# Long convolution by matrix DFT: transforms folded mod 4, its products shared between two engines, filter taps on row halves of the array

## What is computed

```python
def two_sided_fftconv(u, h_fwd, h_bwd):
    L = u.shape[1]
    filt = jnp.concatenate([h_fwd, jnp.zeros((1, h_fwd.shape[1]), F32), h_bwd[1:][::-1]], axis=0)
    filt_f = jnp.fft.rfft(filt, n=2 * L, axis=0)
    u_f = jnp.fft.rfft(u.astype(F32), n=2 * L, axis=1)
    y = jnp.fft.irfft(u_f * filt_f[None], n=2 * L, axis=1)[:, :L]
    return y.astype(u.dtype)

def hyena_mixer(u, w_in, b_in, conv_w, conv_b, f_w1, f_b1, f_freq1, f_w2, f_b2, f_freq2, f_w3, decay, d_bias, w_out, b_out):
    L = u.shape[1]
    z = dwconv3(u @ w_in + b_in, conv_w, conv_b)
    x1, x2, v = jnp.split(z, 3, axis=-1)
    h_fwd, h_bwd = hyena_filters(L, f_w1, f_b1, f_freq1, f_w2, f_b2, f_freq2, f_w3, decay)
    v = v * x2
    y = (two_sided_fftconv(v, h_fwd, h_bwd) + v * d_bias) * x1
    return y @ w_out + b_out
```

## Time and profile before

| | |
|---|---|
| median of three runs | 1707.78 us (1706.72 to 1708.12) |
| the profiled execution, its own time | 1708.62 us |
| its span | 1706.8 us |
| PE busy | 1686.2 us, 99% |
| DVE busy | 1038.0 us, 61% |
| POOL busy | 1019.2 us, 60% |
| ACT busy | 560.6 us, 33% |
| PE's granted clock, mean | 0.996 |

### The profile page before, as it was taken

One profiled execution on the slowest core, in us unless ns is written; L12 is line 12 of the kernel. 1 busy time (PEld: TensorE's weight loads), 2 busy tenths in 40 slices (PEclk: granted clock), 3 DMA queues, 4 the chain that ended last, 5 costly groups with the idle time before them and its releaser, 6 DMA issues.

```text
span 1706.8 us, 24447 instructions
## 1 busy us (share of the span) xinstructions
PE 1686.2 (99%) x9142; PEld 1402.0 (82%) x9142; DVE 1038.0 (61%) x1514; ACT 560.6 (33%) x1019; POOL 1019.2 (60%) x675
## 2 busy tenths in 40 slices
PE   9999999999999999999999999999999999999998
PEld 7778888788888887789888888888888898887887
DVE  3457767677777863445477637756548548846173
ACT  3557777624233232203223125232222221113111
POOL 3437676565666764555666175666667645557663
PEclk8999999999999999999999999999999999999999
DMA  9213233132259862343432133334443344222332
GB/s 357 78 56 108 100 105 103 35 111 76 94 201 314 289 224 92 125 147 120 165 99 87 37 100 100 118 122 153 143 134 121 126 161 150 86 74 93 99 99 87
DMA packets 56760, 217.20 MB, mean 127 GB/s; under 512 B 6305, under 2 KB 8609, under 8 KB 53346
## 3 DMA queue, kind: packets, MB, share of 16 engines
q1 hardware_dynamic: 51634, 201.80, 35.0%
q10 hardware_dynamic: 5040, 14.22, 2.2%
HBM read 201.84 MB, written 14.16 MB: 127 GB/s over the span
## 4 chain that ended last, share of the span: by engine, by line
PE 92%; DVE 4%; ACT 1%; POOL 1%; DMA 1%; issue 0%; SPq 0%; DVEq 0%; POOLq 0%; ACTq 0%
PE PS L2036 27%; PE PS L2037 26%; PE PS L2038 26%; PE PS L2367 2%; PE PS L2383 2%; PE PS L786 2%; PE PS L573 1%; PE PS L2190 1%; PE PS L1434 1%; DMA X<-in_x 0%; DVE WA L1634 0%; PE PS L1440 0%; POOL WL L1954 0%; POOL PR L1979 0%; PE PS L2105 0%
## 5 line engine op out<-in xcount | busy, mean ns | idle before, releaser
L1954 POOL TENSOR_TENSOR WL<-RAW,WH 128x1024 fp32r<-128x1024 f32 (+3 forms) x233 | 601.1, 2580 | 19.5
L2036 PE MATMUL PS<-HH,WH 128*128 128x512 f32 (+1 forms) x1400 | 529.5, 378 | 2.8 <-POOL WL L1954 1.1
L2038 PE MATMUL PS<-HH,WL 128*128 128x512 f32 (+1 forms) x1400 | 524.7, 375 | 0.0
L2037 PE MATMUL PS<-HL,WH 128*128 128x512 f32 (+1 forms) x1400 | 524.5, 375 | 0.0
L1951 POOL TENSOR_SCALAR WH<-RAW 128x1024 fp32r<-128x1024 f32 (+3 forms) x233 | 258.1, 1108 | 295.6 <-PE PS L2038 280.4
L2036 PEld LDWEIGHTS PS<-HH,WH 128*128 128x128 f32 x1400 | 263.6, 188 | 57.5 <-issue 10.1
L2038 PEld LDWEIGHTS PS<-HH,WL 128*128 128x128 f32 x1400 | 263.5, 188 | 47.7
L2037 PEld LDWEIGHTS PS<-HL,WH 128*128 128x128 f32 x1400 | 263.6, 188 | 45.8
L1950 POOL TENSOR_TENSOR SC<-ONES 1x1 f32<-1x1 f32 x134 | 32.1, 239 | 281.8 <-PE PS L2038 281.8
L1979 POOL TENSOR_SCALAR PR<-PR,SC 128x768 f32<-128x768 f32 x47 | 109.5, 2337 | 69.8 <-DVE SC L3080 69.8
L2036 PE MATMUL PS<-HIDH,WH 128*128 128x512 f32 (+1 forms) x396 | 148.4, 375 | 0.0
(11 more groups left out here) (435 smaller groups left out, 2778.8 us busy)
## 6 DMA issues: line engine op xcount, KB each, us to landing
RAW<-in_wup SPq DMA_DIRECT2D x88, 512.0 KB, 3.5
MRF<-in_modw SPq DMA_DIRECT2D x52, 512.0 KB, 4.6
RAW<-in_wdn SPq DMA_DIRECT2D x32, 704.0 KB, 4.1
MR<-in_modw SPq DMA_DIRECT2D x28, 512.0 KB, 3.5
RAW<-in_whin SPq DMA_DIRECT2D x28, 512.0 KB, 3.5
MK<-in_modk SPq DMA_DIRECT2D x8, 1024.0 KB, 9.9
RAW<-in_whead SPq DMA_DIRECT2D x8, 640.0 KB, 4.9
RAW<-in_wo SPq DMA_DIRECT2D x8, 512.0 KB, 3.5
```

The costliest lines, as they stand in the source:

```text
L1954: pool.tensor_tensor(WL[s][:, 0:n], raw[:, 0:n], WH[s][:, 0:n].bitcast(F32), ALU.subtract).then_inc(tile_split, 1)
L2036: pe.matmul(out, wh, xh, start=first, stop=False)
L2037: pe.matmul(out, wh, xl, start=False, stop=False)
L2038: return pe.matmul(out, wl, xh, start=False, stop=last)
```

## The change

The signal is folded mod 4. The four residues of the times 0, 2, 1, 3 mod 4 (RESIDUE) are transformed separately for 128 frequencies (`transform(c, odd)`: 4 x 1 x 3 matmuls), with one tile of cosines and sines (`vdft`) that is loaded once into DFT_RAW, split by POOL and kept in place 3. Sums and differences of these give the spectrum at all 512 frequencies (`even_sums`, `odd_sums`, `first_sums`). The multiplications by HS are shared: DVE has the second class (`second_class`), POOL the first (`first_class`), but for the last two sums of class 1; `joined` adds them. `mixed` gives eight sums per chunk that undo the folding, done by POOL for the first chunk and by DVE for the second. The inverse (`back(c, k)`) has the table G as stationary operand: 2 matmuls of 512 columns for each residue, with times on partitions; ACT copies the result to YT, and `turn_back` transposes it, 4 transposes for each of eight channel tiles. The output projection's first two tiles are interleaved with them, and the split of y for the first four channel tiles goes to UTH and UTL. From input tile 11 on ACT writes WH (`rounded`) and POOL only WL (`rest`). The four spectrum tiles are no longer in the ring of weights. For the filters, the two matmuls of a tap use 64 rows each: forward in bank 6, backward in bank 7; DVE windows both (the backward one to BACK in SBUF) and forms difference and sum. FW3N and the two ACT instructions that made it go. In the filter tiles the second half of the frequencies is in falling order.

```diff
 def input_at(n):
 
-    return FIRST_TILE["hyin"] + n + sum(n > m for m in SPECTRUM_AFTER)
+    return FIRST_TILE["hyin"] + n
...
+            sp.dma_start(DFT_RAW[:, :], a["vdft"]).then_inc(S["tab_in"], 16)
             for c in range(4):
                 ring("hyin", a["whin"], 4 + c)
                 sp.dma_start(HS[:, c, :, :].rearrange("p s n -> p (s n)"), d_hs[:, c, :]).then_inc(S["g_in"], 16)
-            for c in range(2):
-                ring("hyin", a["whin"], 8 + c)
-                sp.dma_start(G[:, 2 * c:2 * c + 2, :], a["idft"][:, 2 * c:2 * c + 2, :]).then_inc(S["g_in"], 16)
...
+            def rest(n):
+
+                t = input_at(n)
+                pool.wait_ge(tile_hi, t + 1)
+                pool.tensor_tensor(WL[place_of(t)][:, 0:D], RAW[t % 2][:, 0:D], WH[place_of(t)][:, 0:D].bitcast(F32),
+                                   ALU.subtract).then_inc(tile_split, 1)
+
+            def first_class(i, part):
+
+                hr1, hi1, x, y = HS[:, i, 0, :], HS[:, i, 1, :], SUM[i % 2][0][:, :], SUM[i % 2][1][:, :]
+                p, q = PROD[0][:, :], PROD[1][:, :]
+                if part == 0:
+                    pool.wait_ge(S["zd"], 5 * (i // 2) + 2 + i % 2)
...
+                    pool.tensor_tensor(p, x, hr1, ALU.mult).then_inc(S["cls"], 1)
+                    pool.tensor_tensor(q, y, hi1, ALU.mult).then_inc(S["cls"], 1)
+                if part == 1:
+                    pool.wait_ge(S["cls"], (CLASS_DONE[i - 1] if i else 0) + 2)
+                    pool.tensor_tensor(x, x, hi1, ALU.mult).then_inc(S["cls"], 1)
+                    pool.tensor_tensor(y, y, hr1, ALU.mult).then_inc(S["cls"], 1)
+                if part == 2:
+                    pool.wait_ge(S["cls"], CLASS_DONE[i] - 2)
+                    pool.tensor_tensor(hr1, p, q, ALU.subtract).then_inc(S["cls"], 1)
+                    pool.tensor_tensor(hi1, y, x, ALU.add).then_inc(S["cls"], 1)
...
+            rest(22)
+            first_class(2, 1)
+            rest(23)
+            first_class(2, 2)
+            for part in range(3):
+                first_class(3, part)
...
-                for half, w in enumerate((FW3, FW3N)):
-                    m = pe.matmul(bank(6 + half), H2T[:, times(k)], w[:, 512 * c:512 * c + 512], start=True, stop=True)
+                for half in range(2):
+                    r = slice(HID_F * half, HID_F * half + HID_F)
+                    m = pe.matmul(bank(6 + half), H2T[r, times(k)], FW3[r, 512 * c:512 * c + 512], start=True, stop=True)
...
-                ins = dve.tensor_tensor(bank(6), bank(6), WN[n % 2][:, :], ALU.mult)
+                dve.tensor_tensor(BACK[:, :], bank(7), WN[n % 2][:, :], ALU.mult)
+                link(dve.tensor_tensor(bank(6), bank(6), WN[n % 2][:, :], ALU.mult))
+                dve.tensor_tensor(bank(7), bank(6), BACK[:, :], ALU.subtract).then_inc(S["pq"], 1)
+                ins = dve.tensor_tensor(bank(6), bank(6), BACK[:, :], ALU.add)
...
-                dve.tensor_tensor(bank(7), bank(7), WN[n % 2][:, :], ALU.mult).then_inc(S["pq"], 1)
...
+                for b in (0, 2, 1, 3):
+                    k = 2 * odd + b % 2
+                    if c and not odd and b == 1:
+                        pe.wait_ge(S["zd"], 5)
+                    m = mm3(bank(2 + b), *chunk(DFT_PLACE, 4 * odd + b), UTH[:, k, :], UTL[:, k, :], True, True)
+                m.then_inc(S["dft"], 1)
+
+            def back(c, k):
+
+                pe.wait_ge(S["mix"], 8 * c + 4 * (k // 2) + 4)
...
+                for wave, x in enumerate(back_terms(c, k)):
+                    m = pe.matmul(bank(back_bank(c, k)), G[:, 2 * k + wave, :], x, start=wave == 0, stop=wave == 1)
+                m.then_inc(S["dft"], 1)
+
+            def turn_back(n):
...
+                pe.wait_ge(S["hcopy"], 8 + 4 * c + 4)
+                if n >= 2:
+                    pe.wait_ge(S["iev"], n - 1)
+                for k, r in enumerate(RESIDUE):
+                    m = pe.transpose(PS[:, 6 + n % 2, r * P:r * P + P], YT[c][:, k, ct * P:ct * P + P], IDENT[:, :])
+                m.then_inc(S["tv"], 1)
...
+            for k in range(4):
+                back(0, k)
+            back(1, 0)
+            back(1, 1)
+            turn_back(0)
+            turn_back(1)
+            back(1, 2)
+            back(1, 3)
+            turn_back(2)
+            turn_back(3)
+            for k in range(3):
+                out_step(0, k)
+            turn_back(4)
+            turn_back(5)
...
+            def rounded(n):
...
+                act.copy(WH[place_of(t)][:, 0:D], RAW[t % 2][:, 0:D]).then_inc(tile_hi, 1)
...
+            def mix():
+                dve.wait_ge(S["zd"], 10)
+                for n in range(8):
+                    out, x, y, op = mixed(1, n)
+                    dve.tensor_tensor(out, x, y, op).then_inc(S["mix"], 1)
+                    dve.wait_ge(S["mix"], 8 + n + 1)
...
             short_conv(22)
-            product(3, 0)
+            joined(2)
             short_conv(23)
-            product(3, 1)
-            product(3, 2)
+            joined(3)
+            mix()
             gated(0)
```

More of the change, by code:

```diff
@@ L553, in pool_hyena, with mix @@
+            def mix(n0, n1):
+                if n0 == 0:
+                    pool.wait_ge(S["zd"], 5)
+                for n in range(n0, n1):
+                    out, x, y, op = mixed(0, n)
+                    pool.tensor_tensor(out, x, y, op).then_inc(S["mix"], 1)
+                    pool.wait_ge(S["mix"], n + 1)
             for j in range(4):
                 split("hyin", j)
-            with pool.Fori(0, 12) as i:
-                for j in range(2):
-                    split("hyin", 4 + j, i, 2)
+            split("hyin", 4)
@@ new lines, in pool_hyena @@
+            dft_hi()
+            split("hyin", 5)
+            dft_lo()
+            with pool.Fori(0, 2) as i:
+                for j in range(2):
+                    split("hyin", 6 + j, i, 2)
+            split("hyin", 10)
+            for n in range(ROUNDED_BY_ACT, 14):
+                rest(n)
+            first_class(0, 0)
+            rest(14)
+            first_class(0, 1)
+            rest(15)
+            first_class(0, 2)
+            rest(16)
+            first_class(1, 0)
+            rest(17)
@@ L798, in pe_hyena @@
             turn_values(3)
+            transform(0, 0)
             into(10)
-            spectra(0)
-            for n in range(11, 15):
+            transform(0, 1)
+            for n in range(11, 17):
                 into(n)
-            spectra(1)
-            into(15)
-            into(16)
             turn_values(4)
@@ new lines, in odd_sums, with odd_banks, first_sums @@
+            def odd_sums(c):
+                dve.wait_ge(S["dft"], 2 * c + 2)
+                dve.wait_ge(S["hcopy"], 4 * c + 4)
+                for b, t in ((2, SUM[0][0]), (4, SUM[0][1])):
+                    dve.tensor_tensor(bank(b + 1), bank(b), t[:, :], ALU.subtract)
+                    ins = dve.tensor_tensor(bank(b), bank(b), t[:, :], ALU.add)
+                link(ins)
+            def odd_banks(i):
+                return (bank(5), bank(3)) if i % 2 else (bank(2), bank(4))
+            def first_sums(i):
+                ao, bo = odd_banks(i)
+                for even, odd, out in zip(EVEN[i % 2], (ao, bo), SUM[i % 2]):
+                    dve.tensor_tensor(out[:, :], even[:, :], odd, ALU.add)
+                    ins = dve.tensor_tensor(odd, even[:, :], odd, ALU.subtract)
+                ins.then_inc(S["zd"], 1)
+                dve.wait_ge(S["zd"], 5 * (i // 2) + 2 + i % 2)
@@ L969, in gated @@
-                y = bank(BACK_BANK[n % 4]).rearrange("p (two s) -> p two s", two=2)
+                x = X1[:, n, :].rearrange("p (u four) -> p four u", four=4)
+                y = bank(6 + n % 2).rearrange("p (four u) -> p four u", four=4)
                 dve.tensor_tensor(x, y, x, ALU.mult).then_inc(S["iev"], 1)
```

336 lines of the change are left out of this document (203 added, 133 removed), and 2 rows, old and new, of the table STAGES.

## The result

The changed kernel takes 1694.1 us (median of four runs, 1693.34 to 1694.58), where the kernel before took 1707.81 beside it (1706.72 to 1708.12). The ratio to it is 0.992, with a 95% interval of 0.9903 to 0.9938. The profiled execution took 1694.43 us with a span of 1692.6, against 1708.62 and 1706.8 before. The forecast was 1693.4 for the median and 1694.2 for the profiled execution, range 1685 to 1702.

What follows compares the result with a forecast made beforehand. PE, busy for 99% of the span, was taken as the bound. Forward transforms -10.9, tail -1.4, middle waits +1.7, taps -5.3 and clock +1.5 gave -14.4: 1694.2 us profiled, 1693.4 median, range 1685 to 1702.

Steps and rivals of the forecast that it cites:

- Forward transforms: Spectrum tiles on PE: 48 matmuls instead of 96, at 0.227 us each, saving 10.9 us.
- Taps: Filter taps on PE: row halves overlap, a pair costs 0.86 + 0.2 us, saving 5.3 us; bounds 0 and 6.9.
- Middle waits: Input tiles' stretch: DVE's products and sums, at 0.725 us each, come late and cost PE 1.7 us; bounds 0 and 3.
- POOL fits, at 90%: From tile 11 on: POOL's 70 us of work, with products and sums at 1.3 us, fits PE's 78 us.
- Rival D: POOL bounds the middle: above 1.56 us per instruction, every 0.1 costs 3 us; 10%, of which slower 4.
- Tail, waits for the sums: Before the second chunk's inverse: PE waits 6.2 us as DVE's sums wait for POOL's splits; bounds 2.6 and 7.4.
- a sum of 37.9: Inverse and first two output tiles: PE's work plus waits, 37.9 us against 39.27 before.
- The step of four elements: Transposes read and gating writes with a stride of four instead of two: priced at nothing, at most 0.6 us.
- 1.8 us of waits for the split tiles: First three output steps: PE waits 1.8 us for inputs that DVE delivers at 1.41 us per channel tile.
- Clock: Behind PE's tail wait: the granted clock may fall, costing up to 5.1 us; 1.5 taken.
- Rival C: Clock at 1.2 GHz for 10 us after the wait, or row halves not overlapping: 1697 to 1702, 12%.
- Rival B: Tail hides: DVE's sums don't wait for POOL (wait 2.6), no clock loss, row halves at 6.9; 1685 to 1688, 18%.

Runs made afterwards that it cites:

- after: The changed kernel's profiled execution, against the kernel before: 1694.43 us; its repetition, the same kernel profiled once more, 1692.4 us.
- pool_rounds: Changed kernel with the rounding of input tiles 11 to 23 given back from ACT to POOL: 1701.03 us, ratio 0.9962 to the kernel before.
- hold: Changed kernel with one more wait on POOL: output tiles are split only after the second chunk's eight sums; 1691.03 us, ratio 0.9905 to the kernel before.
- fill: Changed kernel with twenty unused fp32 matmuls on PE ahead of its wait for the sums: 1692.04 us, ratio 0.9909 to the kernel before.
- gate_time: Changed kernel with DVE's gating walking X in steps of one and PSUM in steps of 128 elements: 1692.01 us, ratio 0.9914 to the kernel before.
- turn_strided: Changed kernel with transposes writing every fourth PSUM element, so gating is contiguous on both sides: 1692.47 us, ratio 0.9916 to the kernel before.
- all_three: early_gate with gate_time's gating order and ACT rounding the first two output tiles: 1685.25 us, ratio 0.9878 to the kernel before.
- early_gate: hold with the second chunk's sums in two parts, two channel tiles gated between, PE and ACT reordered: 1688.07 us, ratio 0.9889 to the kernel before.
- hold_turn: hold with the first two transposes back moved ahead of the second chunk's inverses on PE: 1690.03 us, ratio 0.9895 to the kernel before.
- before: The kernel before the change, unedited: profiled execution 1708.62 us; profiled once more, 1706.05 us.

## Why the prediction was right

It came out within 0.7 us, with its mechanism: PE's saved work is won in A, and what is saved on the inverse is given back in a tail in which DVE's sums wait for POOL. That the number came so close is in part luck: wrong terms of nearly the same size cancel, on the taps and in the middle, and once more inside the tail. Its terms, one by one:

- **Forward transforms, -10.9.** Measured as A without the taps: 14.58 - 3.56 = 11.0.
- **Taps, -5.3.** This is the term that was mis-sized on PE. Overlap was right: 0.80 us of 0.86, near the ideal, as in the two blocks that it was read from. The charge for the switch of shape was too low. The pair saves 0.43 to 0.44 us, 3.5 in all, not 0.66. I had charged 0.2 for the switch because the blocks of the earlier trace rows show 0.2 to 0.4 over the ideal. Here one excursion to the other shape and back costs 0.37 to 0.4, the upper end of that: 0.2 of it inside the block (1.07 against 0.86), 0.2 in the first full matmul behind it (0.43 instead of 0.23). That matmul was not in my count.
- **Middle waits, +1.7.** Measured 0: PE busy for 112.80 of 112.80 us. I priced DVE's instructions at 0.725 each, which is what a chain has when each step waits for the one before. DVE's independent ones start 0.60 apart (chain of after, 931.80 to 933.00), so there was more slack than my hand layout had. That this is why no wait came is argued from the distances; no run shows it. This term and the taps' error cancel: 1.7 too much against 1.8 too much gain.
- **POOL fits, at 90%.** Right: no wait for POOL in the middle with 27 of its 30 instructions at 1.27 to 1.31 us and three at 1.75, where I took 1.3; with 13.5 us more (pool_rounds) it is late. Rival D was close but not reached.
- **Tail, waits for the sums 6.2.** Measured 5.5, released by a sum into HS, with three of four sums over 1 us. hold shows the cause. It was 0.7 shorter: POOL's last product ended 0.45 sooner after tile 23 than I had it (931.09 less 927.84 is 3.25, not 3.7), and from there to the fourth sum it took 9.20 instead of 9.4. DVE's earlier join won nothing, since its first sum waits for POOL's split anyway. (The bound of 7.4 for this wait comes to 7.2 by its own terms.) Without the clock B would be 38.10 by fill, against a sum of 37.9. Inside that sum two errors cancel: all waits together were taken at 9.4 us and are 8.6, the work at 28.5 and is 29.4.
- **The step of four elements, "at nothing, at most 0.6".** This was the wrong step, and it is hidden in that agreement. It costs nothing on PE, and I had weighed it only as PE's work. It costs DVE 8 x 0.39 = 3.1 us in the one stretch where DVE sets the pace; 1.0 to 1.2 of it reached the end (B of gate_time and turn_strided against after; PE's waits fell by 1.2). I had put DVE's gating at 0.72, as it was before. From that I forecast 1.8 us of waits for the split tiles, and 1.9 came, but with the gating really at 0.69 (gate_time) they are 0.7: the term was met only because the step that I left out made up for waits that I had too long.
- **Clock, +1.5, up to 5.1.** Measured 2.45 (fill); the repetition of after, with 5.9 us of work at 1.2 GHz, paid 0.4 more. Rival C's clock, 10 us at 1.2 GHz, did not come: it was 6.8 us.
- **Rival B, 1685 to 1688.** Its premise, sums that don't wait for POOL, is false for the change as made. Its time is what all_three reaches, 1685.25, by taking away that wait, the step of four and the clock's fall, and by making the sums in two parts.

So of the 14.2 us of the two profiles, 13.4 belong to the change (14.58 less 1.15), and 0.8 to the start and the end, where I had forecast nothing. Against -14.4 the change was over-forecast by 1.0: 1.8 too much on the taps, 1.7 too little for the middle, and 1.0 too little for the tail with its clock (+1.15 against +0.1).

Left open is why the clock falls in hold, at a place where PE has just waited twice for 2.5 us together, and not in early_gate, which has three waits of up to 1.2. No run separates the lengths of waits from their spacing.

## What to carry to other kernels

When an engine is relieved, look at who must deliver next: here 10 us of PE work came off the inverse and none of it was won until DVE's eight sums and POOL's weight splits no longer ran against each other. An engine that works ahead of need can be told to wait. By the medians, each against the kernel before in its own session, this one line (hold) was worth 2.6 us (4.2 on the landmarks of its fastest execution), against 3.5 for the row halves. A changed step in an access pattern must be priced on every engine that walks it, and an excursion to another tile shape on the instruction behind it too.

## What was unexpected of the hardware

- **A DVE sum of two SBUF operands waits for POOL even if POOL's instruction has only one input.** The second sum ended 0.55 us behind the 1.03 us rounding (L2166), just as the others behind the two-input splits. Sums with one operand in PSUM were not held by the same kind of POOL instruction. POOL pays too: in after the split beside such sums took 2.66 us, where the other 18 of its width between 815 and 945 us took 2.36 to 2.42, and a marker of one element took 0.64 instead of 0.19. "GPSIMD Engine Reference" of the Trainium skill, section Specifications, names the contention for VectorE instructions with two SBUF inputs; that part agrees.
- **A step of 16 bytes in SBUF costs DVE 57%** (1.08 against 0.69 us for 512 elements), a step of 8 bytes, as in the kernel before, nothing (0.688). "SBUF — State Buffer" of the Trainium skill, section "Door 1: The DMA port swizzle", describes lines of 16 bytes that want at least two hits each, with which these three numbers agree; it also gives 4 fp32 as how far one can step for free, and a step of four was not free here. The same note says of PSUM that non-contiguous access slows matmuls significantly. Transposes that wrote every fourth element took 0.87 us for eight records, as contiguous ones did in after, and DVE read PSUM in steps of 128 elements at 0.69. For these the measurement decides; no run here tries it on another kind of matmul.
- **The clock after a wait.** In after the clock fell to 1.2 GHz during the wait of 5.5 us and stayed there for 6.8 us, 5.1 of them behind the wait, worth 2.45 us. In pool_rounds a wait of 2.3 us was followed by 3.4 us of it, and hold and hold_turn had 3.4 us each. At the start of the kernel 3.4, 6.8 or 10.2 us of it occur in executions of one and the same program (3.4 and 10.2 in before), which makes up to 3 us of difference between runs.
